# A streaming encoder step: two token differences moved from GpSimd to VectorE, one weight sum moved from VectorE to adding DMAs, and the queues reordered around them

## The chip, the cores and the metric

One core of one Trainium2 chip runs the whole program. The metric is the device time of that core in microseconds; before the change the median of three runs is 1407.86 us. Times below that carry a position, such as 317.2, are microseconds from the first instruction of one profiled execution.

## What is computed

Two layers of a hybrid encoder are applied to 640 tokens: 512 frames of one new stream and 16 frames of each of 8 running streams. All data is float32. Cut to what matters here:

```python
def hybrid_layer(x, ...):
    n = rms_norm(x, ln1_w)
    proj = n @ w_in                       # retention and short convolution use slices of proj
    ...
    x = x + concat([ret_out, conv_out]) @ w_out
    h2 = rms_norm(x, ln2_w)
    x = x + square(relu(h2 @ w_up)) @ w_down     # w_up (1024, 4096), w_down (4096, 1024)
    return x, r_new, new_buf
```

The change lies where the second half of a layer begins: at the product with `w_out` (its end) and the first block of `h2 @ w_up`.

## The kernel before

Each matrix product runs on TensorE with operands split into a high and a low part (both fp32r), as three matmuls: high by high, high by low, low by high. ScalarE makes the high part by a copy, VectorE the low part by subtracting the high part from the raw data. So every operand passes ScalarE, then VectorE, then TensorE.

The products with `w_out`, `w_up` and `w_down` are done by blocks called **quads**: 1 for `w_out` (quad 0), then for each of four blocks b of 512 by 512 quarters an up quad (2b+1) and a down quad (2b+2). A quad has four raw weight quarters of 1 MB, named 11, 12, 21 and 22, in four slots of `raws`. It is multiplied in Winograd's form, with **seven** products and not eight, each of sums and differences of quarters. In order they are B11, B21, SUM_1112, SUM_111222, SUM_1222, B22, SUM_ALL. An **item** is one product's weight: item = 7 * quad + product. It is split in two halves h = 0, 1 (`weight_half(item, h)`: ScalarE at line 1141, VectorE at line 1755) into a ring of two places, so that item n may be written when product n - 2 has been multiplied. Items of the first up quad are 7 (B11), 8 (B21), 9 (SUM_1112), 10, 11, 12 and 13.

The sums of weights come about in two ways. `weight_sum` (line 1765) is a VectorE addition in place: 11 += 12 gives SUM_1112, then 11 += 22 gives SUM_111222. `add_onto` (line 1474) is a DMA issued by GpSimd that adds a quarter from memory onto one that lies in `raws`: 12 += 22 for SUM_1222, once SUM_1112 has been made of the raw 12, and 11 += 21 for SUM_ALL.

The token side of the first up quad needs sums too, made once per layer since all four blocks b share them. Each is a tile of 128 x 1280. The normalised tokens are turned by TensorE (`turn`, line 703), tile by tile, and read by ScalarE (lines 968 to 973) and VectorE (lines 1546 and 1548), which also makes the first difference `t_diff` (named s_raw in the profile, as the next three are). Then GpSimd makes the second difference `s2_raw` = t_diff - t11 (line 1488) and the third `t21` = t11 - t21 (line 1489), and VectorE the fourth, `s4_raw` (`last_difference`, line 1844). Each is split by `in_diff_hi_of(n)` on ScalarE (line 1230) and `in_diff_lo_of(n)` on VectorE (line 1854 for n = 0, line 1852 for the others), with n = 0, 1, 2, 3 for products SUM_1112, SUM_111222, SUM_1222 and B22.

TensorE runs `up_half` (line 808), 24 matmuls for each product and half. Before a half it waits for its weights (`half_lo`), for its tokens (`in_diff_lo`), and for its PSUM banks: SUM_1112's half h goes to the bank that B21's half h leaves, when VectorE has added that to `hidden` (`hidden_sum`, line 1780). Copies of products by ScalarE (`copy_product`, line 1163) free the others.

Each engine runs its own list in the order in which the code stands; nothing is reordered. The order in the first up quad is written out by hand, in the branch `b == 0` of `up` on ScalarE and on VectorE. On GpSimd it is the loop over quads, with the row factors of the tokens (`row_rstd`, lines 1371 and 1374) in quad 0. On SyncE each load of a quad's quarters waits for the last low part made of what lies in its slot.

## Time and profile before

| | us |
|---|---|
| median of 3 runs | 1407.86 |
| lowest and highest | 1407.82 and 1409.0 |
| the profiled execution | 1408.8 |
| its span, first to last instruction | 1407.1 |

The two layers run the same instructions; what happens at 317 us in the first stands at 1012 us in the second. A row of a timeline gives start, duration, engine, line, operation and count, and in brackets the idle time before it and what ended that. "PE" is TensorE's matmuls, "DVE" VectorE, "ACT" ScalarE, "POOL" GpSimd, "SPq" the queue of SyncE. Start to start, VectorE's instructions in a row come 0.08 us sooner than their durations add up to, since one begins while the one before it drains.

### The profile page before, as it was taken

The page shows a single profiled execution, that of the slowest core. Times are in us where ns is not written, and L with a number is a line of the kernel's source. Part 1 is how long each engine was busy: PE and PEld are TensorE (multiplying, and loading weights), DVE is VectorE, ACT ScalarE, POOL GpSimd, SP SyncE. Part 2 cuts the span into 40 slices and gives each one's busy share as a digit, 9 for nine tenths or more (in the row PEclk, how much of TensorE's full clock was granted, in tenths as well). Part 3 has the DMA queues.
Part 4 walks back from the last instruction along what each step waited for, and adds up shares of the span by engine and source line. Part 5 has one row for each costly group of instructions (what it writes and reads, how often), then busy time and mean ns, then how long its engine had stood idle before and what let it go on. Part 6 is the DMA issues. An engine that isn't in the chain of part 4 may idle for free.

```text
span 1407.1 us, 21462 instructions
## 1 busy us (share of the span) xinstructions
PE 1377.2 (98%) x7702; PEld 1236.7 (88%) x7702; DVE 947.0 (67%) x1144; ACT 618.1 (44%) x736; POOL 191.4 (14%) x193
## 2 busy tenths in 40 slices
PE   8999999998999999999999999999899999999997
PEld 6888999888889899899878889998798998998986
DVE  5336415988975966867861473278889678688586
ACT  5311221466636446446543012134574464464463
POOL 2343200021000000000032430000400000000001
PEclk9999999999999999999999999999999999999999
DMA  7424203525454645555142242054166455544623
GB/s 273 135 76 121 83 1 128 134 84 122 110 159 121 145 100 142 146 118 158 31 138 96 90 121 68 3 158 140 46 150 150 103 142 145 120 120 120 150 60 105
DMA packets 93728, 162.39 MB, mean 115 GB/s; under 512 B 3956, under 2 KB 21492, under 8 KB 93624
## 3 DMA queue, kind: packets, MB, share of 16 engines
q1 hardware_dynamic: 74472, 123.18, 26.0%
q0 software_dynamic: 19008, 37.75, 15.8%
q8 instruction: 66, 1.08, 0.3%
q14 instruction: 38, 0.31, 0.1%
q10 hardware_dynamic: 144, 0.07, 0.0%
HBM read 153.58 MB, written 7.41 MB: 114 GB/s over the span
## 4 chain that ended last, share of the span: by engine, by line
PE 94%; DVE 2%; issue 2%; ACT 1%; POOL 1%; DMA 0%; DVEq 0%; SPq 0%; POOLq 0%; ACTq 0%
PE pair L808 27%; PE pair L867 25%; PE pair L653 15%; PE pair L663 12%; PE pair L880 8%; PE pair L703 2%; PE pair L741 1%; PE pair L748 1%; PE pair L722 1%; DVE ring L1755 1%; DVE x L1801 1%; PE pair L726 1%; PE pair L731 1%; DMA w_raw<-in_w_in 0%; PE pair L734 0%
## 5 line engine op out<-in xcount | busy, mean ns | idle before, releaser
L808 PE MATMUL pair<-mlp_in_hi,ring 128*128 128x320 f32 x1792 | 400.1, 311 | 9.8 <-DVE hidden L1780 9.8
L1141 ACT ACTIVATE ring<-raws 128x1024 fp32r<-128x1024 f32 x248 | 259.8, 1057 | 290.1 <-PE pair L867 150.2
L867 PE MATMUL pair<-ring,a_ring 128*128 128x512 f32 x1632 | 380.4, 390 | 0.0
L1755 DVE TENSOR_TENSOR ring<-raws,ring 128x1024 fp32r<-128x1024 f32 x248 | 305.2, 1241 | 101.6 <-ACT ring L1141 100.1
L867 PEld LDWEIGHTS pair<-ring,a_ring 128*128 128x128 f32 x1632 | 305.5, 188 | 63.6
L808 PEld LDWEIGHTS pair<-mlp_in_hi,ring 128*128 128x128 f32 x1792 | 302.7, 189 | 11.2 <-DVE ring L1755 10.3
L808 PE MATMUL pair<-mlp_in_lo,ring 128*128 128x320 f32 x896 | 278.2, 310 | 0.0
L808 PEld LDWEIGHTS pair<-mlp_in_lo,ring 128*128 128x128 f32 x896 | 169.6, 189 | 0.2
L663 PE MATMUL pair<-norm_hi,ring 128*128 128x320 f32 x512 | 114.5, 310 | 0.0
L1801 DVE TENSOR_TENSOR x<-x,pair 128x512 f32<-128x512 f32 x160 | 103.3, 678 | 11.4 <-PE pair L867 11.4
L653 PE MATMUL pair<-ring,norm_hi 128*128 128x512 f32 x320 | 101.6, 399 | 3.2 <-DVE norm_lo L1563 3.1
L653 PE MATMUL pair<-pair_a,norm_hi 128*128 128x512 f32 x320 | 101.0, 397 | 0.0
L880 PE MATMUL pair<-ring,sample_mid_hi 128*128 128x512 f32 x304 | 94.6, 392 | 0.0
L1765 DVE TENSOR_TENSOR raws<-raws 128x1024 f32<-128x1024 f32 x72 | 87.1, 1221 | 4.2
L663 PEld LDWEIGHTS pair<-norm_hi,ring 128*128 128x128 f32 x512 | 85.8, 188 | 0.1
L663 PE MATMUL pair<-norm_lo,ring 128*128 128x320 f32 x256 | 79.1, 309 | 0.0
L1474 POOL DMA_DIRECT2D raws<-in_w_mlp_down x16 | 20.7, 1295 | 391.4 <-DVE raws L1765 226.0
L653 PEld LDWEIGHTS pair<-ring,norm_hi 128*128 128x128 f32 x320 | 59.5, 191 | 16.0 <-DVE norm_lo L1563 2.0
L653 PEld LDWEIGHTS pair<-pair_a,norm_hi 128*128 128x128 f32 x320 | 58.9, 188 | 12.3 <-issue 1.0
L880 PEld LDWEIGHTS pair<-ring,sample_mid_hi 128*128 128x128 f32 x304 | 57.1, 188 | 12.6
L1780 DVE TENSOR_TENSOR hidden<-hidden,pair 128x640 f32<-128x640 f32 x48 | 39.3, 818 | 41.6 <-PE pair L808 41.6
L1816 DVE TENSOR_TENSOR a_ring<-hidden,a_ring 128x1024 fp32r<-128x1024 f32 x50 | 60.9, 1218 | 4.1 <-ACT a_ring L1216 4.1
(153 smaller groups left out, 1686.2 us busy)
## 6 DMA issues: line engine op xcount, KB each, us to landing
raws<-in_w_mlp_up SPq DMA_DIRECT2D x32, 1024.0 KB, 5.3
raws<-in_w_mlp_down SPq DMA_DIRECT2D x32, 1024.0 KB, 5.0
w_raw<-in_w_in SPq DMA_DIRECT2D x27, 1024.0 KB, 6.1
raws<-in_w_mlp_up POOLq DMA_DIRECT2D x16, 1024.0 KB, 9.1
raws<-in_w_mlp_down POOLq DMA_DIRECT2D x16, 1024.0 KB, 8.8
raws<-in_w_out SPq DMA_DIRECT2D x8, 1024.0 KB, 8.4
past_state<-in_state_ret SPq DMA_DIRECT2D x8, 512.0 KB, 4.5
out_ret_s<-past_state SPq DMA_DIRECT2D x8, 512.0 KB, 4.9
```

What stands on the lines that cost most here:

```text
L653: mm = pe.matmul(out, act[a][:, k, tile * P:(tile + 1) * P], w_of(b, n), start=(n == 0 and m == 0), stop=(n == len(ks) - 1 and m == 2))
L663: mm = pe.matmul(out, w_of(chunk, k // 4, a)[:, k % 4, ft * P:(ft + 1) * P], norms[b][:, k, half * HALF:(half + 1) * HALF], start=(k == 0 ...
L703: mm = pe.transpose(out[:, i * P:(i + 1) * P], src[i], identity)
L808: mm = pe.matmul(out[:, n, 0:HALF], item_half(item, h, a)[:, k, n * P:(n + 1) * P], mlp_in[i][c][:, k], start=(i in (B11, B21, SUM_1112, B ...
L867: mm = pe.matmul(out[:], a_item[:, a, 2 * h + k, pair * P:(pair + 1) * P], item_half(item, h, c)[:, k], start=(i in (B11, B21, SUM_1112) a ...
L880: mm = pe.matmul(sample_bank[:], sample_mid[part][a][:, k], item_half(item, k // 2, c)[:, k % 2], start=(i in (B11, SUM_1222) and (k, m) = ...
L1141: nc.scalar.activation(item_half(item, h, 0), raw_half(quad, RAW_OF[i], h), ACT.Copy).then_inc(half_hi.sem, 1)
L1755: nc.vector.tensor_tensor(item_half(item, h, 1), raw_half(quad, RAW_OF[i], h), f(item_half(item, h, 0)), ALU.subtract).then_inc(half_lo.se ...
L1765: nc.vector.tensor_tensor(out, out, raw_half(quad, name, h), ALU.add).then_inc(weights_summed.sem, 1)
L1780: nc.vector.tensor_tensor(hh, hh, src, ALU.add).then_inc(hidden_summed.sem, 1)
L1801: nc.vector.tensor_tensor(xx, xx, src[:], op).then_inc(x_added.sem, 1)
L1816: nc.vector.tensor_tensor(a_ring[:, n % 2, 1], src, f(a_ring[:, n % 2, 0]), ALU.subtract).then_inc(a_lo.sem, 1)
```

## The change

1. `s2_raw` and `t21` are made by VectorE (`next_difference`, `third_difference`) and not by GpSimd.
2. For quad 1, product SUM_1112 alone, VectorE's two additions 11 += 12 go. GpSimd issues two DMAs (`add_half`) in their place, each adding half of quarter 12 (512 KB, rows of 256 floats) from memory onto the half of 11 in `raws`, once the B11 item's half has been split. Each half has a semaphore of its own, `first_summed`, on which ScalarE's `weight_half(9, h)` waits. The DMA 12 += 22 of quad 1, which had waited for the additions, now waits only until quarter 12 is loaded, and stands right behind the second half in the queue.
3. The first half's DMA stands between the row factors of tiles 2 and 3, the second's behind those of tile 4.
4. The lists of ScalarE and VectorE for the first up quad are reordered.

```diff
+BY_DMA = (1, SUM_1112)
@@ ScalarE, weight_half
+                    elif (quad, i) == BY_DMA:
+                        act.wait_ge(first_summed[h].sem, first_summed[h].at(layer, 16))
@@ ScalarE, up(0)
                         read_tile(3)
                         weight_half(item + 1, 1)
+                        weight_half(item + 2, 0)
                         read_tile(4)
                         in_diff_hi_of(0)
-                        weight_half(item + 2, 0)
+                        weight_half(item + 2, 1)
                         copy_product(b, B11, 1)
+                        weight_half(item + 3, 0)
                         in_diff_hi_of(1)
-                        weight_half(item + 2, 1)
-                        weight_half(item + 3, 0)
-                        in_diff_hi_of(2)
                         copy_product(b, SUM_1112, 0)
-                        copy_product(b, SUM_1112, 1)
                         weight_half(item + 3, 1)
+                        copy_product(b, SUM_1112, 1)
+                        in_diff_hi_of(2)
                         weight_half(item + 4, 0)
+                        weight_half(item + 4, 1)
@@ GpSimd
+                def add_half(h):
+                    quad, i = BY_DMA
+                    pool.wait_ge(half_lo.sem, half_lo.at(layer, 2 * (quad * PRODUCTS + B11) + h + 1))
+                    settle(pool)
+                    pool.dma_start(raw_half(quad, "11", h), quad_weights(layer, quad, "12")[:, :, h * 256:(h + 1) * 256],
+                                   accum_op=ALU.add).then_inc(first_summed[h].sem, 16)
                 for quad in range(QUADS):
-                    pool.wait_ge(weights_summed.sem, weights_summed.at(layer, sums_to(quad, SUM_1112, 1)))
+                    if quad == BY_DMA[0]:
+                        slot = slot_of(quad, "12")
+                        pool.wait_ge(slot_in[slot].sem, slot_in[slot].at(layer, 16 * (quad + 1)))
+                    else:
+                        pool.wait_ge(weights_summed.sem, weights_summed.at(layer, sums_to(quad, SUM_1112, 1)))
                     add_onto(quad, "12", "22", onto_12)
@@ GpSimd, in quad 0
-                        for t in range(NT):
+                        for t in range(3):
                             row_rstd(layer, NT, t)
-                        last = TURN["n2", NT - 1, 1]
-                        pool.wait_ge(turn_lo.sem, turn_lo.at(layer, split_turns_to(last)))
-                        nc.gpsimd.tensor_tensor(s2_raw[:], t_diff[:], t11[:], ALU.subtract).then_inc(s2_ready.sem, 1)
-                        nc.gpsimd.tensor_tensor(t21[:], t11[:], t21[:], ALU.subtract).then_inc(s3_ready.sem, 1)
+                        add_half(0)
+                        for t in range(3, NT):
+                            row_rstd(layer, NT, t)
+                        add_half(1)
@@ VectorE
+                def next_difference():
+                    nc.vector.tensor_tensor(s2_raw[:], t_diff[:], t11[:], ALU.subtract).then_inc(s2_ready.sem, 1)
+                def third_difference():
+                    dve.wait_ge(s2_ready.sem, s2_ready.at(layer, 1))
+                    nc.vector.tensor_tensor(t21[:], t11[:], t21[:], ALU.subtract).then_inc(s3_ready.sem, 1)
```

VectorE, the first up quad, from the factors applied to tokens of tile 3 on. The names: xn is a normalised tile, `ring<-raws,ring` a weight half, `raws<-raws` a weight sum, `hidden` a hidden sum, `s_raw<-...` a difference. Before:

```order
L1765 TENSOR_TENSOR raws<-raws 128x4x256
L1854 SCALAR_TENSOR_TENSOR mlp_in_lo<-s_raw_102,mlp_in_hi 128x1280
L1754 REGISTER_ALU
L1755 TENSOR_TENSOR ring<-raws,ring 128x1024
L1772 REGISTER_ALU
L1777 ISA
L1780 TENSOR_TENSOR hidden<-hidden,pair 128x2x320
L1765 TENSOR_TENSOR raws<-raws 128x4x256
```

and now, from the same place (behind the last piece read of tile 4):

```order
L1773 TENSOR_TENSOR ring<-raws,ring 128x1024
L1880 SCALAR_TENSOR_TENSOR mlp_in_lo<-s_raw_102,mlp_in_hi 128x1280
L1790 REGISTER_ALU
L1795 ISA
L1798 TENSOR_TENSOR hidden<-hidden,pair 128x2x320
L1772 REGISTER_ALU
L1773 TENSOR_TENSOR ring<-raws,ring 128x1024
L1780 REGISTER_ALU
L1783 TENSOR_TENSOR raws<-raws 128x4x256
L1790 REGISTER_ALU
L1795 REGISTER_ALU
L1798 TENSOR_TENSOR hidden<-hidden,pair 128x2x320
```

The first sum is gone, the weight half of item 9 stands ahead of the low part of the tokens, and both halves of item 9 stand ahead of the second hidden sum. The two differences follow behind these rows.

GpSimd, from the row factors of the last tile (`var`, `rstd`) on, before:

```order
L1371 TENSOR_SCALAR var<-sums 128x1 [waits squares]
L1373 REGISTER_ALU
L1374 TENSOR_TENSOR rstd<-var,minus_half 128x1 [waits eps_step]
L1487 ISA
L1488 TENSOR_TENSOR s_raw_103<-s_raw_102,t_72 128x1280 [waits turn_lo]
L1489 TENSOR_TENSOR s_raw_100<-t_72,s_raw_100 128x1280
L1478 REGISTER_ALU
L1474 ISA [waits weights_summed]
L1474 DMA raws<-in_w_mlp_up 128x4x512
```

and now:

```order
L1378 TENSOR_SCALAR var<-sums 128x1 [waits squares]
L1380 REGISTER_ALU
L1381 TENSOR_TENSOR rstd<-var,minus_half 128x1 [waits eps_step]
L1487 REGISTER_ALU
L1489 ISA [waits half_lo]
L1489 DMA raws<-in_w_mlp_up 128x4x256
L1495 ISA
L1481 ISA [waits slot_in1]
L1481 DMA raws<-in_w_mlp_up 128x4x512
```

The differences have left the list, and the second half's DMA and the whole quarter's stand next to each other. The lists of TensorE and SyncE are the same as before.

## Rows read from the trace of the kernel before

**Rows 1.** The page, part 1: busy time, share of the span, instructions.
```profile
PE 1377.2 (98%) x7702; PEld 1236.7 (88%) x7702; DVE 947.0 (67%) x1144; ACT 618.1 (44%) x736; POOL 191.4 (14%) x193
```

**Rows 2.** Waits of TensorE: us in total, times, longest.
```profile
PE pair L808 <- DVE hidden L1780: 9.8, 2, 4.9
```

**Rows 3.** Timeline of TensorE, first layer (columns as told above).
```profile
309.80 0.66 PE L703 MATMUL pair<-const,xn 128*128 128x128 f32 x4 [0.94 <-DVE s_raw L1548]
...
316.75 0.46 PE L808 MATMUL pair<-mlp_in_hi,ring 128*128 128x320 f32 x2
...
317.19 0.31 PE L808 MATMUL pair<-mlp_in_hi,ring 128*128 128x320 f32 x1
322.41 0.63 PE L808 MATMUL pair<-mlp_in_hi,ring 128*128 128x320 f32 x1 [4.91 <-DVE hidden L1780]
...
325.43 0.45 PE L808 MATMUL pair<-mlp_in_hi,ring 128*128 128x320 f32 x2
```

**Rows 4.** Timeline of TensorE, second layer: the same place.
```profile
1016.71 0.63 PE L808 MATMUL pair<-mlp_in_hi,ring 128*128 128x320 f32 x1 [4.91 <-DVE hidden L1780]
```

**Rows 5.** Windows: length; busy (count) of PE, PEld, DVE, ACT, POOL; clock; DMA.
```profile
322.41:325.43 3.02, 3.02 (x12) 3.02 (x13) 2.63 (x3) 1.06 (x1) 1.21 (x1) 0.52 0.02 5
...
1016.71:1021.81 5.10, 5.10 (x20) 5.10 (x20) 4.71 (x5) 1.56 (x2) 1.33 (x1) 0.52 0.26 35
```

**Rows 6.** Timeline of VectorE, first layer, 304 to 318 us.
```profile
304.14 1.28 DVE L1528 SCALAR_TENSOR_TENSOR xn<-x,rstd,norm_row 128x1024 f32<-128x1024 f32 x1 [0.71 <-POOL rstd L1374]
306.13 1.28 DVE L1528 SCALAR_TENSOR_TENSOR xn<-x,rstd,norm_row 128x1024 f32<-128x1024 f32 x1 [0.71 <-POOL rstd L1374]
...
311.74 0.68 DVE L1548 TENSOR_TENSOR s_raw<-s_raw,pair 128x512 f32<-128x512 f32 x1
...
313.76 3.98 DVE L1854 SCALAR_TENSOR_TENSOR mlp_in_lo<-s_raw,mlp_in_hi 128x1280 fp32r<-128x1280 f32 x1 [0.21 <-ACT mlp_in_hi L1230]
317.66 3.89 DVE L1755 TENSOR_TENSOR ring<-raws,ring 128x1024 fp32r<-128x1024 f32 x1
```

**Rows 7.** Timeline of GpSimd, first layer, 294 to 325 us.
```profile
294.14 0.54 POOL L1374 TENSOR_TENSOR rstd<-var,minus_half 128x1 f32<-128x1 f32 x1
...
304.19 1.28 POOL L1371 TENSOR_SCALAR var<-sums 128x1 f32<-128x1 f32 x1
305.56 0.54 POOL L1374 TENSOR_TENSOR rstd<-var,minus_half 128x1 f32<-128x1 f32 x1
312.49 3.89 POOL L1488 TENSOR_TENSOR s_raw<-s_raw,t 128x1280 f32<-128x1280 f32 x1 [6.40 <-DVE s_raw L1548]
316.35 4.12 POOL L1489 TENSOR_TENSOR s_raw<-t,s_raw 128x1280 f32<-128x1280 f32 x1
324.22 1.33 POOL L1474 DMA_DIRECT2D raws<-in_w_mlp_up  x1 [3.75 <-DVE raws L1765]
```

**Rows 8.** Groups of VectorE, 300 to 345 us: busy, mean ns; idle.
```profile
L1765 DVE TENSOR_TENSOR raws<-raws 128x1024 f32<-128x1024 f32 x4 | 4.9, 1217 | 0.0
...
L1844 DVE SCALAR_TENSOR_TENSOR s_raw<-t,s_raw 128x1280 f32<-128x1280 f32 x1 | 1.5, 1485 | 0.0
```

**Rows 9.** Timeline of ScalarE, first layer, 307 to 313 us.
```profile
307.24 1.06 ACT L1141 ACTIVATE ring<-raws 128x1024 fp32r<-128x1024 f32 x1
...
312.45 1.28 ACT L1230 ACTIVATE mlp_in_hi<-s_raw 128x1280 fp32r<-128x1280 f32 x1 [1.35 <-DVE s_raw L1548]
```

**Rows 10.** Timeline of SyncE's queue, 311 us.
```profile
311.03 27.12 SPq L505 DMA_DIRECT2D raws<-in_w_mlp_down  x2
```

**Rows 11.** DMA issues: KB, median us to landing; then line 1474's.
```profile
raws<-in_w_mlp_up POOLq DMA_DIRECT2D x16, 1024.0 KB, 9.1
...
DMA to landing us min/median/max: 8.3/9.1/15.1
```

**Rows 12.** DMA queues, 326:334 and 141:145: packets, MB, share of 16.
```profile
q0 software_dynamic: 528, 1.05, 77.7%
...
q1 hardware_dynamic: 1040, 0.52, 46.0%
```

More of the change, by code:

```diff
@@ L419, in program @@
         half_lo = Signal("half_lo", 2 * ITEMS)
-        weights_summed = Signal("weights_summed", QUADS * len(SUMS))
+        weights_summed = Signal("weights_summed", QUADS * len(SUMS) - 2)
+        first_summed = [Signal(f"first_summed{h}", 16) for h in range(2)]
         onto_12 = Signal("onto_12", 16 * QUADS)
```

31 lines of the change are left out of this document (16 added, 15 removed).

## The prediction

> **What bounds the kernel.** Read the busy shares first: TensorE is busy for 98% of the span, all others far less [rows 1], so only time in which TensorE stands still, or runs slowly, can be won. Next its waits: one pair stands out, 9.8 us in two waits of 4.9, on VectorE's hidden sum [rows 2]. Then its timeline around each. In both layers TensorE ends B21 and stands before SUM_1112's first half. In the first layer the last matmul starts at 317.19, one more would have started at 317.34 (three take 0.44, from 316.75 to 317.19), and the next comes at 322.41: 5.07 us lost [rows 3]; the second layer has the same 4.91 us of idle [rows 4]. Then come slow matmuls: 11 start from 322.41 until 325.43 (the window counts 12, one of them the one before the edge or at it), and 19 from 1016.71 until 1021.81, at a mean clock of 0.52, nearly all at the lower of its two levels (1.2 GHz) [rows 3, 4, 5]. At 0.147 us each they would take 1.61 and 2.79 us, and they take 3.02 and 5.10, so 1.41 and 2.31 us more. Before it stood still the engine had run at that full pace. The whole price of the place is 2 x 5.07 + 1.41 + 2.31 = **13.86 us**.
>
> **Why VectorE is late there.** Its low part of t_diff took 3.98 us and the weight half behind it 3.89 [rows 6]. The same instruction form on the same shape takes 1.49 [rows 8], and a weight half has the shape and operands of a sum, 1.22 [rows 8]. During both, GpSimd made its two differences, 312.49 to 320.47 [rows 7]. The times fit turns taken, not shared: 316.38 (GpSimd's end) + 1.49 = 317.87, against 317.74 measured. So 2.49 + 2.67 = 5.16 us of VectorE's time is waiting for GpSimd, and a sum of 1.22 stood ahead of them.
>
> **What the change takes off and puts on VectorE**, per layer: off two sums, 2 x 1.22 = 2.44, and the 5.16 of waiting; on two differences of 1.49 each (two inputs of 128 x 1280, priced by the nearest row, the fourth difference, line 1844 [rows 8]), 2.98. Net 4.6 us less, and what is added stands behind what TensorE waits for first.
>
> **The new order followed through the first layer.** I use starts, each step being its duration less 0.08: weight half or sum 1.14, low part or difference 1.40, hidden sum 0.73 (the form takes about 0.81), half a read of a turned tile 0.60.
>
> Tile 3 is normalised at 304.14 [rows 6]; now the weight half (8, 0) follows at 305.34. GpSimd's factor for tile 4 was computed at 305.56 while VectorE idled [rows 6, 7]; its forerunner, begun at 304.19, took 1.28 us beside a VectorE instruction [rows 7]. So I take it that the factor now waits until 306.5 and ends at 307.05, and that tile 4 is normalised at 307.2, not 306.13. Tile 3's low parts start at 308.4 and 309.0. TensorE's last turn waits for the second of them: it started at 309.80 [rows 3], now at 309.73. Tile 4's low parts start at 311.06 and 311.67, against 311.74 for the second [rows 6]. This stretch gains 0.07 us; if the factor slips in earlier, it gains up to 0.3.
>
> Then VectorE: weight half (9, 0) at 312.3; low part of t_diff at 313.7 (ScalarE's high part starts 0.71 behind 311.67, at 312.4, and takes 1.28 [rows 9]); hidden sum 0 at 315.1; weight half (9, 1) at 315.8; sum at 317.0; hidden sum 1 at 318.1, behind B21's second half (its last matmul starts at 317.1); second difference at 318.8; weight half (10, 0) at 320.2; low part 1 at 321.7; sum at 323.1; third difference at 324.2; weight half (10, 1) at 325.6; low part 2 at 327.1; (11, 0) at 328.5.
>
> TensorE, if never stopped, starts SUM_1112's halves at 317.3 and 320.8, SUM_111222's at 324.3 and 327.8, SUM_1222 at 331.4 (24 matmuls of 0.147 are 3.52 us). What each needs is done at 315.9, 318.9, 323.1, 326.8 and 329.7. The margins are 1.4, 1.9, 1.2, 1.0 and 1.7 us, and by the same steps B22, due at 338.4, has its tokens at 335.4. So the stall goes whole, unless a DMA is late. What is late next is VectorE's (10, 1), with 1.0 us.
>
> **The two adding DMAs.** The first half is issued behind tile 2's factor, which ends at 294.68 [rows 7], with nothing to stop tile 3's factor at 303; it may take the longest landing seen, 15.1 us [rows 11], and be there at 311. ScalarE reaches it at 308.2, behind the half that started at 307.24 [rows 9]. At the median it costs nothing. Its ends: 0, or up to 2.5 us of ScalarE, with tile 4's reads queued behind it.
>
> The second half decides. Tile 4's factor ends at 307.05. A release came 0.8 us before the DMA's start in the one row that shows it (a sum ended at 323.4, the DMA started at 324.22 [rows 7]), so it starts at about 307.9. ScalarE waits for it with (9, 1), and behind that wait stand its copy of B11 and all of SUM_111222's weights; VectorE's queue waits with it. Weight half (9, 1) at 315.8 wants it landed by **314.6**; with the margin of 1.0, TensorE loses nothing up to **315.6**, and one us for each beyond. No row shows an adding DMA of 512 KB. Upper end: as long as the whole, 9.1 us [rows 11], plus contention with SyncE's load issued at 311.03 [rows 10], taken as 1.5: landed at 318.5. Lower end: packets cost by size. An adding packet of 2 KB costs 0.777 x 16 x 8 / 528 = 0.188 us, 33 per engine 6.2 us; a plain one of 512 B costs 0.46 x 16 x 4 / 1040 = 0.028 us, and a plain one of 2 KB some 0.09 (half the 0.188, since adding reads the destination too: an estimate from these two rows) [rows 12]. So cost goes by size, half the bytes take 3.1 us less, and 9.1 becomes 6.0: landed at 313.9. I take 6 to 7, landed at 314 to 315, since the packet rows are nearest. No stall.
>
> This change splits one large transfer where there was none. The Trainium skill, "DMA: Bandwidth & Descriptors", "Anatomy of one DMA — SWDGE (gpsimd) path", speaks against small ones: a fixed 2.0 us and then bytes at 436 GB/s, which makes 512 KB cost 0.73 of 1 MB. On the 9.1 us measured that would be 6.6 us, landed at 314.5, by an estimate from that page; its own figure for 1 MB, 4.4 us, is half of what this trace has for an adding DMA, so the trace does not agree with its size.
>
> The DMA 12 += 22 now goes out at 309.2 and not at 324.22 [rows 7]; it is wanted at 327. It costs nothing unless it shares the queue with the half in front of it (below).
>
> **The sum.** 1408.8 of the profiled execution - 13.9 = 1394.9. The median lies 0.9 under that execution, so **1394.0**, 0.98% less.
>
> **Rivals.**
>
> *The half is late, or VectorE is over its margins* (0.20). Either the DMA lands at 316 to 318.5, or a step is dearer than priced. One way is that the 3.98 us is this instruction's own cost, with its factor of -1 and fp32r output, and not GpSimd's doing: 2.49 us more, less 1.0 of margin, is 1.5 a layer. Against it: line 1844 has two inputs and such a factor at 1.49 [rows 8]. With the DMA at its upper end it is 318.5 - 315.6 = 2.9 a layer. That gives 1394.0 + 3.0 to 5.8 = 1397 to 1399.8.
>
> *The same time as before* (0.04). A landing at 321 gives back what is won.
>
> *Slower* (0.04). The half and the 1 MB behind it in GpSimd's queue are drained together, not one after the other. Then the half lands with the whole: 307.9 + 9.1 + 3.1, and 3 us more for SyncE's load, is 323. TensorE then stands for 7.4 us where it stood for 5.07, with the same slow clock behind: +2.3 a layer, so 1407.9 + 4.6 = 1412.5. It decides from a landing at about 320.7. For it: no row shows two of GpSimd's DMAs one right behind the other, and one alone took 15.1 [rows 11]. Against it: the half is 1.3 us ahead, the time its descriptors take to be written [rows 7].
>
> **Chances.** Stall gone whole: 0.70, 1393 to 1395.5. Late or dear: 0.20. As before: 0.04. Slower: 0.04. The rest, 0.02, is a wait elsewhere, of which I see none, since all later work hangs on TensorE's pace. What a measurement of this kernel can tell from no change is about 0.2%, 2.8 us. Faster 0.92, same 0.04, slower 0.04. The range reaches up over most of the second case, 1398.5, and down to 1392.8, for the turns' waits (0.94 us a layer [rows 3]) falling with the rest.
>
> **What would show it.** Right: no wait of TensorE on line 1780's successor, no stretch at half clock near 322 and 1016 less the shift, low part of t_diff at 1.5 us, second half's landing before 315.6, both differences at 1.4 to 1.5 us on VectorE. Wrong: a TensorE wait behind ScalarE's weight half (9, 1), which is the DMA; a wait at SUM_111222, which is VectorE's load; a VectorE instruction there still near 4 us, which is a GpSimd instruction or something else holding it.

## The result

The changed kernel takes **1393.47 us** (median of 4 runs, 1393.14 to 1394.05), against 1408.43 for the kernel before in the runs beside it (4 runs, 1407.82 to 1413.44). The ratio is **0.9888 [0.987, 0.9905]**: faster by 1.1%. The forecast was 0.98% (1394.0 of 1407.86, a ratio of 0.9902). It lies within the interval of the ratio. But the ratio times 1407.86 is 1392.1, and that lies 0.7 us below the low end of the range, 1392.8. How far outside depends on one run: the median itself, 1393.47, lies inside the range, and the kernel before has a run of 1413.44 beside three of 1407.82 to 1409.0. The quotient of the two medians is 0.9894; that of the means is 0.9887, and 0.9896 without that run, which would be 1393.2. The direction and the mechanism hold. The gain is larger than the sum's 13.9 us, by 1.1 us between the medians (14.96) and by 1.9 us by the ratio.

The profiled execution of the changed kernel took 1394.05; its span is 1392.4, 14.7 less than before.

### The profile after

The page of the changed kernel, part 1 (busy time, share of the span, instructions), to be laid beside [rows 1]:

```profile
PE 1372.0 (99%) x7702; PEld 1232.0 (88%) x7702; DVE 937.7 (67%) x1144; ACT 617.5 (44%) x736; POOL 182.4 (13%) x193
```

TensorE's waits in the changed kernel, over the whole span (us in total, times, longest). The group of [rows 2], 9.8 us in two waits, is gone, and nothing of the first up quad has taken its place; what is left there is the wait for the turned tiles, on line 1566. Three of the five rows:

```profile
PE pair L644 <- DMA x<-in_x_sample: 4.9, 1, 4.9
PE pair L658 <- DVE norm_lo L1581: 3.4, 2, 2.1
PE pair L708 <- DVE s_raw L1566: 2.3, 4, 0.6
```

VectorE's timeline in the changed kernel, first layer, from the weight half (9, 0) on (start, duration, engine, line, operation, count, and in brackets the idle time before it with what ended that). Line 1773 is the weight half, 1880 and 1878 are the low parts of the tokens, 1860 and 1865 the two differences that came from GpSimd:

```profile
311.36 1.22 DVE L1773 TENSOR_TENSOR ring<-raws,ring 128x1024 fp32r<-128x1024 f32 x1
312.79 1.49 DVE L1880 SCALAR_TENSOR_TENSOR mlp_in_lo<-s_raw,mlp_in_hi 128x1280 fp32r<-128x1280 f32 x1 [0.21 <-ACT mlp_in_hi L1237]
...
315.23 1.23 DVE L1773 TENSOR_TENSOR ring<-raws,ring 128x1024 fp32r<-128x1024 f32 x1 [0.21 <-ACT ring L1148]
...
318.24 1.49 DVE L1860 TENSOR_TENSOR s_raw<-s_raw,t 128x1280 f32<-128x1280 f32 x1
...
321.07 1.49 DVE L1878 TENSOR_TENSOR mlp_in_lo<-s_raw,mlp_in_hi 128x1280 fp32r<-128x1280 f32 x1 [0.21 <-ACT mlp_in_hi L1237]
...
323.62 1.48 DVE L1865 TENSOR_TENSOR s_raw<-t,s_raw 128x1280 f32<-128x1280 f32 x1
```

The low part of t_diff takes 1.49 where it took 3.98, the weight half behind it 1.23 where it took 3.89 [rows 6], and the two differences cost 1.49 and 1.48. No instruction here is near 4 us.

GpSimd's timeline in the changed kernel, first layer: the factors of tile 4, the second half's adding DMA (line 1489), and the whole quarter's (line 1481):

```profile
303.48 1.29 POOL L1378 TENSOR_SCALAR var<-sums 128x1 f32<-128x1 f32 x1
304.85 1.41 POOL L1381 TENSOR_TENSOR rstd<-var,minus_half 128x1 f32<-128x1 f32 x1
306.22 1.34 POOL L1489 DMA_DIRECT2D raws<-in_w_mlp_up  x1
314.35 1.29 POOL L1481 DMA_DIRECT2D raws<-in_w_mlp_up  x1 [6.78 <-issue]
```

The DMA 12 += 22 was expected right behind the half, at about 309. It went out at 314.35, after 6.78 us in which GpSimd waited for nothing that the profile names.

ScalarE's weight half (9, 1), which waits for the second half's DMA, in the first and the second layer of the changed kernel:

```profile
314.13 1.06 ACT L1148 ACTIVATE ring<-raws 128x1024 fp32r<-128x1024 f32 x1 [1.38 <-DMA raws<-in_w_mlp_up]
```

```profile
1002.53 1.06 ACT L1148 ACTIVATE ring<-raws 128x1024 fp32r<-128x1024 f32 x1 [2.01 <-DMA raws<-in_w_mlp_up]
```

So the DMA did end last there, and two views show how close it came. The first is the line of landings of line 1489 in the changed kernel; the second is TensorE's timeline in the second layer, at the matmul where SUM_111222 begins:

```profile
DMA to landing us min/median/max: 6.2/7.1/8.4
```

```profile
1011.03 0.58 PE L813 MATMUL pair<-mlp_in_hi,ring 128*128 128x320 f32 x2
1011.45 0.31 PE L813 MATMUL pair<-mlp_in_lo,ring 128*128 128x320 f32 x1
```

A pair of such matmuls spans 0.46 elsewhere; this one spans 0.58, so TensorE stood for 0.12 us in the middle of it. The landing 8.4 us after the issue in the second layer just used the margin up. In the first layer it landed after 7.8 us, and nothing was lost.

### Where the 14.7 us went

A layer's first up quad is measured from its first matmul to the first matmul of the down quad behind it. For the changed kernel these are two rows of TensorE's timeline, the first and the last of the stretch:

```profile
299.52 0.41 PE L813 MATMUL pair<-mlp_in_hi,ring 128*128 128x320 f32 x1
...
351.56 0.39 PE L872 MATMUL pair<-ring,a_ring 128*128 128x512 f32 x1
```

and for the kernel before:

```profile
300.25 0.41 PE L808 MATMUL pair<-mlp_in_hi,ring 128*128 128x320 f32 x1
...
359.00 0.63 PE L867 MATMUL pair<-ring,a_ring 128*128 128x512 f32 x2
```

The same two places of the second layer stand at 987.30 and 1039.46 in the changed kernel, at 994.55 and 1054.22 in the one before.

| us | before | changed | less |
|---|---|---|---|
| first up quad, layer 1 | 58.75 | 52.04 | 6.71 |
| first up quad, layer 2 | 59.67 | 52.16 | 7.51 |
| from the start to the first of them | 300.25 | 299.52 | 0.73 |
| between them | 635.55 | 635.74 | -0.19 |
| behind them | 352.88 | 352.94 | -0.06 |

The two quads give 14.22. The 0.73 at the start is not the change's: the two programs run the same work there, and a second profile of the kernel before (below) has its first up matmul at 299.49, as early as the changed kernel. In the first profile of before, TensorE ran a stretch from 10 to 16 us at a mean granted clock of 0.72, in that of the changed kernel at 1.00. Windows (length; busy and count of PE, PEld, DVE, ACT, POOL; clock; DMA share; GB/s), before and then changed:

```profile
10.00:16.00 6.00, 5.17 (x20) 4.20 (x20) 5.33 (x8) 4.33 (x9) 1.64 (x3) 0.72 1.04 405
```

```profile
10.00:16.00 6.00, 4.55 (x23) 3.64 (x24) 5.38 (x8) 4.45 (x9) 1.65 (x3) 1.00 1.04 407
```

### The profile page after: what moved, and what is told of

Its sections match the earlier page's. It is cut to its first block, busy times and chain, and to the rows that moved or that the text cites. A ratio compares the mean times of both kernels' runs of the same rounds, so it can differ in the third digit from the quotient of the medians.

```text
span 1392.4 us, 21466 instructions
## 1 busy us (share of the span) xinstructions
PE 1372.0 (99%) x7702; PEld 1232.0 (88%) x7702; DVE 937.7 (67%) x1144; ACT 617.5 (44%) x736; POOL 182.4 (13%) x193
## 3 DMA queue, kind: packets, MB, share of 16 engines
HBM read 155.67 MB, written 7.41 MB: 117 GB/s over the span
## 4 chain that ended last, share of the span: by engine, by line
PE 94%; issue 2%; DVE 1%; ACT 1%; POOL 1%; DMA 0%; DVEq 0%; SPq 0%; POOLq 0%; ACTq 0%
PE pair L813 27%; PE pair L872 26%; PE pair L658 15%; PE pair L668 12%; PE pair L885 8%; PE pair L708 2%; PE pair L746 1%; PE pair L753 1%; PE pair L727 1%; PE pair L731 1%; PE pair L736 1%; DVE x L1819 0%; DMA w_raw<-in_w_in 0%; PE pair L739 0%; POOL var L1378 0%
## 5 line engine op out<-in xcount | busy, mean ns | idle before, releaser
L1773 DVE TENSOR_TENSOR ring<-raws,ring 128x1024 fp32r<-128x1024 f32 x248 | 300.1, 1221 | 96.5 <-ACT ring L1148 95.1
L1783 DVE TENSOR_TENSOR raws<-raws 128x1024 f32<-128x1024 f32 x68 | 82.3, 1223 | 4.2
L658 PEld LDWEIGHTS pair<-pair_a,norm_hi 128*128 128x128 f32 x320 | 58.9, 188 | 12.3 <-issue 1.0
```

The costliest lines, as they stand in the source:

```text
L658: mm = pe.matmul(out, act[a][:, k, tile * P:(tile + 1) * P], w_of(b, n), start=(n == 0 and m == 0), stop=(n == len(ks) - 1 and m == 2))
L1773: nc.vector.tensor_tensor(item_half(item, h, 1), raw_half(quad, RAW_OF[i], h), f(item_half(item, h, 0)), ALU.subtract).then_inc(half_lo.se ...
L1783: nc.vector.tensor_tensor(out, out, raw_half(quad, name, h), ALU.add).then_inc(weights_summed.sem, 1)
```

## The experiments

Each is told with its sections: the length of the first up quad in layers 1 and 2, measured as above. "Stall" is an idle time of TensorE in that quad, other than the wait for a turn. Each ratio is against runs of the kernel before that were taken with it on the same chip.

### Both kernels again

> The changed kernel once more, more rounds, to narrow its ratio. Theory A (the gain is the stall at SUM_1112, 13.9 us, plus about 0.5 us of shorter turn waits; the rest of the 14.7 us between the two spans is the start of the program, where the trace of before shows matmuls at the lower clock from 11.4 to 14.8 us and that of the changed kernel none): ratio 0.9893 to 0.9900 where both start alike. Rival B (the change itself gives 15.5 us or more): 0.9888 again.

> The kernel before, unchanged. Theory A: the 3.4 us of lower clock at 11.4 us come and go from run to run; a second profile has the first up matmul anywhere between 299.5 and 300.3 us, and a ratio of 1.000. Rival B: the dip at the start is the same each time, at 300.25 us.

The changed kernel took 1394.78 (1393.39 to 1396.61), the ratio is 0.99 [0.9884, 0.9917]; the one before 1409.05, ratio 1.0007 [0.9997, 1.0017]. This interval holds the ratios of both theories; what decides for the first is the start, 299.49 us, with a clock of 1.00 from 10 to 16 us. The sections of the changed kernel are 52.03 and 52.03, those of before **59.38 and 59.95**, where its first profile had 58.75 and 59.67. The stalls are the same, 4.92 and 4.91. What differs is the slow stretch around the end of the stall. A window of the kernel before, run again, over the stall of layer 1 and what follows; then the same window of its first profile:

```profile
317.00:328.00 11.00, 6.34 (x30) 6.35 (x31) 10.61 (x8) 2.80 (x3) 4.04 (x2) 0.69 0.23 37
```

```profile
317.00:328.00 11.00, 6.09 (x33) 5.83 (x32) 10.61 (x8) 2.73 (x4) 4.80 (x2) 0.84 0.17 24
```

The mean granted clock is 0.69 and not 0.84. The lower level is half of the upper one, so a mean of 0.69 is 2 x 0.31 x 11 = 6.8 us of the 11 at the lower level, where there were 3.5. Part of it lies in the stall itself, where it costs nothing: 2.5 of the 6.8, and 0.5 of the 3.5. Of the rest, 16 matmuls from 321.65 to 326.02 took 4.37 us for 2.35. So the term of 1.41 us of slow matmuls in layer 1, from [rows 5], is 2.02 here, and layer 2's, by its 22 matmuls, is 2.59 against 2.31. By this profile the price of the place is 14.8 us, not 13.86.

The changed kernel's run had a slow stretch too, in another place, in the second layer's first products. Windows of it and of the first profile of the changed kernel:

```profile
705.00:712.00 7.00, 5.87 (x23) 4.82 (x24) 3.84 (x6) 0.79 (x2) 1.42 (x2) 0.76 0.74 270
```

```profile
705.00:712.00 7.00, 6.21 (x31) 5.26 (x32) 4.97 (x7) 2.12 (x4) 1.74 (x4) 1.00 0.70 255
```

It made the way between the two up quads 637.47 instead of 635.74: 1.7 us, with nothing changed in the program.

### Each part alone

The differences on VectorE alone, with the DMAs and sums as before and the lists reordered only around them (the functions `next_difference` and `third_difference` as in the change; GpSimd's two differences removed):

```diff
@@ ScalarE
                         copy_product(b, B11, 1)
-                        in_diff_hi_of(1)
                         weight_half(item + 2, 1)
                         weight_half(item + 3, 0)
-                        in_diff_hi_of(2)
+                        in_diff_hi_of(1)
                         copy_product(b, SUM_1112, 0)
-                        copy_product(b, SUM_1112, 1)
                         weight_half(item + 3, 1)
+                        copy_product(b, SUM_1112, 1)
+                        in_diff_hi_of(2)
@@ VectorE
                         weight_sum(q, SUM_111222, 0)
-                        in_diff_lo_of(1)
+                        next_difference()
                         weight_half(item + 3, 0)
+                        in_diff_lo_of(1)
                         weight_sum(q, SUM_111222, 1)
+                        third_difference()
                         weight_half(item + 3, 1)
```

> The two differences on VectorE, the weight sums left on VectorE as before. By VectorE's steps the low part of the first difference takes 1.49 us, TensorE starts SUM_1112 without a stall (at most 0.2 us), but SUM_111222 waits about 1.8 us a layer for the low part of the second difference: 2 x (6.9 - 1.9) = 10 us saved, 1398 us, ratio 0.993. Rival (the 3.98 us belong to the instruction): low part still near 4 us, ratio 0.997 or more.

1399.85 (1398.05 to 1404.5), ratio 0.9943 [0.9925, 0.9962]; sections 54.22 and 54.22. TensorE's wait before SUM_1112 is gone. One is left, before SUM_111222: first TensorE's waits, then what VectorE did, in the first layer.

```profile
PE pair L808 <- DVE mlp_in_lo L1855: 1.7, 1, 1.7
```

```profile
312.88 1.49 DVE L1857 SCALAR_TENSOR_TENSOR mlp_in_lo<-s_raw,mlp_in_hi 128x1280 fp32r<-128x1280 f32 x1 [0.21 <-ACT mlp_in_hi L1230]
...
323.60 1.49 DVE L1855 TENSOR_TENSOR mlp_in_lo<-s_raw,mlp_in_hi 128x1280 fp32r<-128x1280 f32 x1 [0.21 <-ACT mlp_in_hi L1230]
```

The low part is short at once, at 1.49. Behind it VectorE now has both its own sums and GpSimd's differences, and the second low part comes 1.7 us late. No slow stretch follows. The median lies 1.9 us over the expected 1398, and in the profiled execution the way between the two up quads is 637.44 us, 1.9 us longer than in the first profile of before.

The DMAs and the new order alone, with the differences left to GpSimd:

```diff
                         add_half(1)
+                        last = TURN["n2", NT - 1, 1]
+                        pool.wait_ge(turn_lo.sem, turn_lo.at(layer, split_turns_to(last)))
+                        nc.gpsimd.tensor_tensor(s2_raw[:], t_diff[:], t11[:], ALU.subtract).then_inc(s2_ready.sem, 1)
+                        nc.gpsimd.tensor_tensor(t21[:], t11[:], t21[:], ALU.subtract).then_inc(s3_ready.sem, 1)
@@ VectorE
-                        next_difference()
...
-                        third_difference()
```

> The adding DMAs and the new order, the two differences left on GpSimd. If VectorE and GpSimd take turns, the low part of the first difference takes 3.8 to 4 us again, TensorE stalls about 1.1 us before SUM_1112's first half and 1.4 before its second: 9.3 us saved, 1399 us, ratio 0.9935. If the DMA sum were the main thing: 0.990.

1399.75 (1399.02 to 1402.58), ratio 0.9943 [0.9926, 0.9959]; sections 54.87 and 54.87. TensorE stands for 1.09 and 1.23 us in each layer. VectorE's timeline has the two held instructions:

```profile
312.98 3.98 DVE L1886 SCALAR_TENSOR_TENSOR mlp_in_lo<-s_raw,mlp_in_hi 128x1280 fp32r<-128x1280 f32 x1 [0.21 <-ACT mlp_in_hi L1237]
...
317.61 3.22 DVE L1778 TENSOR_TENSOR ring<-raws,ring 128x1024 fp32r<-128x1024 f32 x1
```

Against the first profile of before, 4.5 and 5.5 us of the two sections go by the first part alone, 3.9 and 4.8 by the second alone, and 6.7 and 7.5 by both: the two gains overlap, and neither part alone clears the place.

### Both parts, but the old order

ScalarE's and VectorE's lists in the first up quad are those of before, with the two differences put between the hidden sums and behind the second sum of SUM_111222. Cut to the moves that the rows below turn on:

```diff
@@ ScalarE
                         weight_half(item + 1, 1)
-                        weight_half(item + 2, 0)
                         read_tile(4)
                         in_diff_hi_of(0)
-                        weight_half(item + 2, 1)
+                        weight_half(item + 2, 0)
                         copy_product(b, B11, 1)
-                        weight_half(item + 3, 0)
                         in_diff_hi_of(1)
+                        weight_half(item + 2, 1)
+                        weight_half(item + 3, 0)
@@ VectorE
-                        weight_half(item + 2, 0)
                         in_diff_lo_of(0)
+                        weight_half(item + 2, 0)
                         hidden_sum(b, B21, 0)
+                        next_difference()
+                        hidden_sum(b, B21, 1)
                         weight_half(item + 2, 1)
                         weight_sum(q, SUM_111222, 0)
-                        hidden_sum(b, B21, 1)
-                        next_difference()
-                        weight_half(item + 3, 0)
                         in_diff_lo_of(1)
+                        weight_half(item + 3, 0)
```

> Both parts of the change, but ScalarE's and VectorE's lists in the order of the kernel before (each difference where its next reader wants it). By the same steps: a stall of 1.3 us before SUM_1112's second half (its weights stand behind the high part of the second difference on ScalarE) and about 4 before SUM_111222's second half: 1405 us, ratio 0.998. If the order is worth little, 1394 us.

1408.74 (1405.27 to 1409.56), ratio **0.9994** [0.9984, 1.0004], sections 59.04 and 59.05: nothing is left of the gain. TensorE's waits in the first up quad of one layer, and ScalarE's timeline there:

```profile
PE pair L813 <- DVE ring L1773: 4.5, 2, 3.4
```

```profile
318.18 1.28 ACT L1237 ACTIVATE mlp_in_hi<-s_raw 128x1280 fp32r<-128x1280 f32 x1 [3.28 <-DVE s_raw L1860]
319.36 1.04 ACT L1148 ACTIVATE ring<-raws 128x1024 fp32r<-128x1024 f32 x1
...
327.90 1.27 ACT L1237 ACTIVATE mlp_in_hi<-s_raw 128x1280 fp32r<-128x1280 f32 x1 [3.93 <-DVE s_raw L1865]
```

The weight half (9, 1) stands behind the high part of the second difference in ScalarE's list. It starts at 319.36, though its DMA had landed by 314.5, where GpSimd issued the next: ScalarE waits 3.28 us in its queue for VectorE to make a difference that TensorE needs only one product later. The half (10, 1) stands in the same way behind the high part of the third difference, for which ScalarE waits 3.93 us, and TensorE stalls 3.44 us before SUM_111222's second half. The stalls, 1.06 and 3.44, add up to about the one of before. The median is 3.7 us over the expected 1405; in both layers TensorE ran slowly behind the longer stall (a mean clock of 0.68 from 332.61 to 336.00).

### Only the length of GpSimd's work

This is the kernel before with one edit that speaks on the mechanism alone: GpSimd still issues both instructions, at the same point, but over one column. It leaves out the rest of both differences, so its outputs are not those of the layer; the second product's tokens and the fourth difference read `t_diff` in place of `s2_raw`, so VectorE and ScalarE do the same amount of work as before.

```diff
-                        nc.gpsimd.tensor_tensor(s2_raw[:], t_diff[:], t11[:], ALU.subtract).then_inc(s2_ready.sem, 1)
-                        nc.gpsimd.tensor_tensor(t21[:], t11[:], t21[:], ALU.subtract).then_inc(s3_ready.sem, 1)
+                        nc.gpsimd.tensor_tensor(s2_raw[:, 0, 0:1], t_diff[:, 0, 0:1], t11[:, 0, 0:1], ALU.subtract).then_inc(s2_ready.sem, 1)
+                        nc.gpsimd.tensor_tensor(t21[:, 0, 0:1], t11[:, 0, 0:1], t21[:, 0, 0:1], ALU.subtract).then_inc(s3_ready.sem, 1)
```

> The kernel before with GpSimd's two differences cut to one column each (the rest of them is left out, and the second one's readers take the first difference), so that GpSimd holds nothing; VectorE's list, its sums and its order are those of before. If GpSimd's 8 us beside VectorE are the whole cause, the low part of the first difference takes 1.49 us, TensorE has no stall over 0.3 us in the first up quad, and first up matmul to first down matmul takes 52.3 us a layer: 1394 us. If VectorE's sums or the order were part of the cause in themselves, 2 us or more of stall stay: 1398 us or more.

1394.12 (1393.77 to 1397.47), ratio **0.9894** [0.9878, 0.9911], sections 52.40 and 52.39, no stall. VectorE's and GpSimd's rows:

```profile
312.46 1.22 DVE L1765 TENSOR_TENSOR raws<-raws 128x1024 f32<-128x1024 f32 x1
313.89 1.49 DVE L1854 SCALAR_TENSOR_TENSOR mlp_in_lo<-s_raw,mlp_in_hi 128x1280 fp32r<-128x1280 f32 x1 [0.20 <-ACT mlp_in_hi L1230]
315.29 1.22 DVE L1755 TENSOR_TENSOR ring<-raws,ring 128x1024 fp32r<-128x1024 f32 x1
```

```profile
312.62 1.11 POOL L1488 TENSOR_TENSOR s_raw<-s_raw,t 128x1 f32<-128x1 f32 x1 [6.40 <-DVE s_raw L1548]
313.69 0.18 POOL L1489 TENSOR_TENSOR s_raw<-t,s_raw 128x1 f32<-128x1 f32 x1
```

With VectorE's sum still ahead of the low part, in the old order, without any DMA of halves, the stall is gone whole (52.3 is what the changed kernel takes with the old wait for the turn, below). **The stall was GpSimd's doing**, all 5 us of it. The sums are free as long as VectorE is not held. This edit also makes GpSimd's results ready at once, and by itself it does not tell a held VectorE from late results. The rows do: in the kernel before the second difference was ready at 316.38 [rows 7], and here ScalarE's weight half (9, 1) waits for VectorE's sum until 318.4 anyway. So it was the holding. GpSimd's first instruction also shows the reverse: one column takes 1.11 us when it is issued under VectorE's sum, and ends at 313.73 with it (313.68); the next takes 0.18.

### GpSimd's work moved by one instruction

The kernel before, with the two differences held until VectorE's first low part is made:

```diff
-                        pool.wait_ge(turn_lo.sem, turn_lo.at(layer, split_turns_to(last)))
+                        pool.wait_ge(in_diff_lo.sem, in_diff_lo.at(layer, 1))
```

> The kernel before with GpSimd's two differences held until the low part of the first one is made. If an instruction that begins first keeps the other out until its end, the low part takes 1.49 us and SUM_1112's first half starts without a stall, but the sum or weight half beside each of GpSimd's instructions takes about 2.5 us more, and TensorE stalls about 3 us before SUM_1112's second half, whose weights stand on ScalarE behind the high part of the second difference: 2 to 4 us a layer saved, 1402 us. If the slow instruction is slow by itself, 1408 us and a low part of 4 us.

1404.79 (1402.32 to 1405.63), ratio 0.9964 [0.995, 0.9978], sections 57.24 and 55.93, a stall of 3.16 before SUM_1112's second half. VectorE's rows and GpSimd's:

```profile
313.12 1.49 DVE L1854 SCALAR_TENSOR_TENSOR mlp_in_lo<-s_raw,mlp_in_hi 128x1280 fp32r<-128x1280 f32 x1 [0.20 <-ACT mlp_in_hi L1230]
...
316.40 3.25 DVE L1765 TENSOR_TENSOR raws<-raws 128x1024 f32<-128x1024 f32 x1
319.57 0.81 DVE L1780 TENSOR_TENSOR hidden<-hidden,pair 128x640 f32<-128x640 f32 x1
320.85 2.64 DVE L1755 TENSOR_TENSOR ring<-raws,ring 128x1024 fp32r<-128x1024 f32 x1 [0.47 <-ACT ring L1141]
```

```profile
314.69 3.87 POOL L1488 TENSOR_TENSOR s_raw<-s_raw,t 128x1280 f32<-128x1280 f32 x1 [9.22 <-DVE mlp_in_lo L1854]
318.53 3.88 POOL L1489 TENSOR_TENSOR s_raw<-t,s_raw 128x1280 f32<-128x1280 f32 x1
```

The low part, the same instruction with its factor and fp32r output, is at 1.49 as soon as no difference runs beside it, and now the plain sum is the one that takes 3.25. The times are those of turns: GpSimd's first ends at 318.56 less some 0.1, plus 1.22, is 319.7 (the sum ends at 319.65); its second ends at 322.41, plus 1.22 is 323.6 (323.49). GpSimd takes turns too: its second difference, recorded from 318.53, stood under the sum until 319.65 and then took 2.8 us, as did the two of the kernel before, counted from the end of the VectorE instruction in front of each (a sum that ended at 313.55, and the low part at 317.74; they end at 316.38 and 320.47). The hidden sum between them, one of whose inputs lies in PSUM, keeps its 0.81 beside a running difference. The Trainium skill, "SBUF — State Buffer", "Who interferes with whom", states this: a VectorE instruction with two SBUF inputs contends with a GpSimd instruction that reads SBUF; one with at most one SBUF input, outside VectorE's 2-port modes, does not; and the shared ports are an exclusive lock, which whoever issues first has for the whole instruction (the page says the last of the 2-port modes). These rows agree with all three.

Of the 3.16 us, some 1.4 are VectorE's second wait (2.64 for 1.22). The rest comes by ScalarE's weight half (9, 1), which starts only at 319.78: it had to wait for the sum, held until 319.65, and for the high part of GpSimd's late difference in front of it, begun at 318.60. The median lies 2.8 us over the expected 1402; behind the stall there was a slow stretch in layer 1 and none in layer 2, whose section is 1.3 us shorter.

### The adding DMAs

The whole quarter's DMA issued ahead of the second half's, which makes the half as late as the slower rival has it:

```diff
                             row_rstd(layer, NT, t)
+                        slot = slot_of(1, "12")
+                        pool.wait_ge(slot_in[slot].sem, slot_in[slot].at(layer, 32))
+                        add_onto(1, "12", "22", onto_12)
                         add_half(1)
```

> The changed kernel with GpSimd's two neighbouring DMAs swapped: the whole quarter (12 += 22) is issued ahead of the second half, so the half is late. GpSimd stood 6.8 to 7.4 us in the changed kernel before its next DMA; if it is held until the DMA in front has landed, the half starts at about 315.6 and lands at 322 to 324, TensorE stalls 7 to 9 us a layer and runs at half clock after it: 1413 us, slower than before (ratio 1.000 to 1.006). If GpSimd is not held, the half starts at 307.6 and lands by 319: a stall of 4 to 5 us, 1404 us.

1416.58 (1412.22 to 1417.81; 1413 was expected), ratio **1.005** [1.0032, 1.0069], sections 63.03 and 61.84, stalls 7.96 and 8.15. GpSimd's rows, and ScalarE's:

```profile
307.12 1.34 POOL L1481 DMA_DIRECT2D raws<-in_w_mlp_up  x1
318.26 1.29 POOL L1489 DMA_DIRECT2D raws<-in_w_mlp_up  x1 [9.80 <-issue]
```

```profile
324.60 1.06 ACT L1148 ACTIVATE ring<-raws 128x1024 fp32r<-128x1024 f32 x1 [10.95 <-DMA raws<-in_w_mlp_up]
```

The price of a late half is as the forecast had it. It gave one us for each us behind a landing of 315.6, and with a landing at 324.5 that is 8.9. But the stall stands before SUM_1112's second half, whose margin was put at 1.9 and not 1.0, so 8.0, and 7.96 idle came. The half is late for another reason than thought, though: it was not drained together with the whole, it was not even issued until the whole had landed, 10.8 us after its start.

So the same kernel as the changed one, with the memory reserved for the descriptors of such DMAs one step larger:

```diff
-    nc = bacc.Bacc("TRN2", target_bir_lowering=False, num_devices=1, dynamic_dma_scratch_size=2048)
+    nc = bacc.Bacc("TRN2", target_bir_lowering=False, num_devices=1, dynamic_dma_scratch_size=2112)
```

> The changed kernel with 2112 bytes and not 2048 of scratch for GpSimd's DMA descriptors, nothing else. Theory: GpSimd is held before the whole quarter's DMA for want of descriptor space; with 64 bytes more that DMA starts at 307.6, 6.7 us sooner. If the queue is drained in order, the half still lands at 314 and the time is that of the changed kernel, 1393.5 us. Rival of the prediction (both drained together): the half lands at 317 to 319 and TensorE stalls 3 us a layer, 1400 us. If space is not the cause, the DMA still starts at 314.35.

1394.47 (1393.88 to 1395.67), ratio 0.9902 [0.9886, 0.9919], sections 52.03 and 52.33. GpSimd's rows, then the DMAs issued from 305 to 330 (KB, median us to landing):

```profile
307.14 1.33 POOL L1489 DMA_DIRECT2D raws<-in_w_mlp_up  x1
307.95 1.85 POOL L1481 DMA_DIRECT2D raws<-in_w_mlp_up  x1
```

```profile
raws<-in_w_mlp_up POOLq DMA_DIRECT2D x2, 1024.0 KB, 12.3
raws<-in_w_mlp_down SPq DMA_DIRECT2D x1, 1024.0 KB, 13.4
raws<-in_w_mlp_up POOLq DMA_DIRECT2D x1, 512.0 KB, 8.2
```

The hold is gone with 64 bytes more: the whole quarter's DMA goes out 0.81 us behind the half's. The half lands 8.2 us after its issue, against 7.8 in the same layer of the changed kernel, and the whole 15.9 us after its own (the 12.3 is the median of this and a later one of 8.8), 8.5 us behind the half. So the queue was drained in its order here, and not both together. In the first layer the 0.4 us cost nothing (52.03), in the second 0.3 us (52.33). As for the time, the larger memory brings nothing, since nobody wants the whole quarter before 327.

### The weight half put ahead of tile 4's normalisation

```diff
                         normalise(layer, NT, 3, ORDER[3], 32)
-                        weight_half(item + 1, 0)
                         normalise(layer, NT, 4, ORDER[4], 32)
+                        weight_half(item + 1, 0)
```

> The changed kernel with tile 4 normalised ahead of weight half (8, 0), as before. One look, by the profile: if the 0.24 us a layer of shorter turn wait come from this exchange, TensorE idles 0.94 us before its last turn again (0.54 in the changed kernel) and first up matmul to first down matmul takes 52.3 us, not 52.05.

One execution, 1393.92, sections 52.30 and 52.29 where the changed kernel has 52.04 and 52.16. The wait for the last turn is 0.95 again, as in [rows 3], not 0.54. This edit of the order is worth 0.25 us a layer, which no measurement of the whole kernel here can tell.

## Why the prediction was right, and where it was not

**What bounds the kernel, and why VectorE was late:** right. The stall, its 5.07 us a layer and the slow matmuls behind it went whole; that this price was taken from too few rows is told below. The reading of 3.98 and 3.89 us as turns taken with GpSimd is shown by the runs with one column and with GpSimd held, and the rival that 3.98 was the instruction's own cost is refuted by the 1.49 of every run that had no difference beside it.

**The prices of the new work:** right. The two differences were put at 1.49 each, from [rows 8], and took 1.49 and 1.48. Step by step the chain came as it was written: the forecast's starts, less the 0.73 by which this execution was ahead, lie within 0.3 us of the rows. The low part of t_diff comes at 312.79 for 313.7 - 0.73 = 312.97, the second difference at 318.24 for 318.07, the third at 323.62 for 323.47.

**The turn gain, 0.07 us a layer:** too small, and left out of the sum, whose 13.9 is the 13.86 of the stall and the slow matmuls alone. TensorE's last turn began at 308.83, which is 9.31 behind its first up matmul at 299.52; it was 309.80 - 300.25 = 9.55 before. That is 0.24, inside the "up to 0.3" that the text allowed if the factor slipped in. The factor did take its turn behind the weight half (1.41 us, 304.85 to 306.26, forecast 307.05 - 0.73 = 306.32); but VectorE took up the normalisation at 306.30 and not at 306.47.

**The second half's DMA:** two steps were wrong and made up for each other. Its issue was put at 307.9, 0.8 us behind the release, from the one row in [rows 7] that had a release to measure. It started at 306.22, right behind the factor, 0.95 earlier than 307.9 - 0.73. And it took 7.8 and 8.4 us, not 6 to 7. The step "cost goes by size", with its 6.0, is near the least that such a half took, 6.2. What was missing in the likeliest value was most likely SyncE's loads, which the forecast counted in its upper end alone: the first halves, issued with no such load beside them, took 6.3 and 6.2, and in the run with the whole quarter first the second halves, issued when those loads were nearly in, took 6.2 and 6.5. No run took the loads away from the second half. The loads are the other issues from 305 to 316:

```profile
raws<-in_w_mlp_down SPq DMA_DIRECT2D x1, 1024.0 KB, 7.0
...
norm_row<-in_norm_rows SPq DMA_DIRECT2D x1, 512.0 KB, 6.5
```

The landing, 306.22 + 7.8 = 314.0, is at the late end of the forecast's 313.3 to 314.3 in this frame. The threshold held to 0.2 us: 315.6 was forecast, 314.9 in this frame, less 0.2 for the earlier turn, so 314.7. The second layer's landing, 994.00 + 8.4 = 1002.4, answers to 1002.4 - (987.30 - 299.52) = 314.6 and lost 0.12 us; the first layer's lost nothing. What came due first was not the weight half (10, 1) but, as far as the rows tell, the low part of the second difference: in layer 2 it ended at 1010.96, 0.3 before the matmul that was late (1011.30), and in layer 1 at 322.56, 0.8 before the same matmul.

**The DMA 12 += 22:** "issued at 309.2" was wrong, and the slower rival's mechanism with it. GpSimd was held 6.78 and 7.41 us behind the half. It cost nothing because it was wanted at 327 and GpSimd had nothing else to do. The rival's price was real, as the run with the whole quarter first shows (1.005); its condition, that both are drained together, came about neither here nor with the larger memory. The rival counted the half 1.3 us ahead; with the larger memory the next DMA started 0.81 us behind it.

**The sum, and the step that failed:** the two sections gave 6.71 and 7.51. The forecast's terms were 5.07 + 1.41 + 0.07 = 6.55 and 5.07 + 2.31 + 0.07 = 7.45. With 0.24 for the turn, and 0.12 taken off in layer 2, they come to 6.72 and 7.50, which is what was measured to 0.01 us. So in the profiled execution the only mis-sized term of the place is the turn gain: 0.48 us where the sum had nothing. The other mis-sized term is the **price of the slow matmuls**: 1.41 + 2.31 = 3.72 was read from one execution, [rows 3 to 5], and another execution of the same kernel has 2.02 + 2.59 = 4.61. It varies by about 1 us, was taken as fixed, and was taken from its cheap side. The later runs point the same way: the three with a stall over 3 us came 2.8 to 3.7 us over their expected times, in which the slow clock was priced low or not at all; the four others for which a time was expected came 0.1 to 1.9 over.

How much of the excess in the medians is this term is not shown, since only two executions of the kernel before have a profile. 13.9 + 0.9 for it, + 0.5 for the turns and - 0.1 for layer 2 is 15.2; the medians of pairs run side by side differ by 14.96 in the first set, 13.08 in the second, and 14.8 for the kernel with one column. That the first is near 15.2 is in part luck.

**The range** was the other failure. Its low end took in 1.2 us, for the turns' waits, and nothing for this term nor for the stretches at lower clock elsewhere: 0.73 at 10 us in the execution that the sum was made against, 1.7 at 707 us in one of the changed kernel. The way between the two up quads, which no edit here touches, takes 635.0 to 636.1 us in eight of the twelve profiles and 637.4 to 638.3 in the other four. Medians of the kernel before are 1407.86 and 1409.05 (14 and 10 runs on one chip), 1409.02 (14) and 1408.89 (8) on two others. A low end of 1391.9, lower by the 0.9 us of the slow matmuls, would have been worked out by an estimate from the second profile. The ratio of the second set, 0.99, would give 1393.8, inside the range: the result stands at the edge of what the runs can tell from the forecast.

**The chances:** 0.70 for the stall gone whole is the case that came; the median of 1393.47 lies in its 1393 to 1395.5, the 1392.1 of the ratio does not. The 0.20 for a late half was not idle, since its margin in layer 2 was below zero by 0.12 us.

## What to carry to other kernels

When two neighbouring rows of VectorE take three times what the same form takes elsewhere, look for GpSimd's instructions beside them and add up its end and their own length; if it fits, move the work by who holds whom, not by who has time left. Removing waits or work from an engine can bring nothing if a list in program order still puts a thing due later ahead of a thing due now: the same two parts gave 1.1% in the new order and nothing in the old. And where a stall's price has a term for the slow clock behind it, read it from both layers and every profile there is, and give the range its spread.

## What the runs showed of the hardware

- The stretch at the lower clock around the end of a stall varies between executions of one kernel: 3.5 us in one and 6.8 in the other at the same stall of 4.9 us in layer 1, with 0.5 and 2.5 us of them inside the stall. Behind stalls of 1.1 to 1.7 us no slow stretch was seen in these runs; behind one of 3.16 there was one in layer 1 and none in layer 2; behind one of 3.44 there was one in both; at 8.0, one of some 10.3, 4.1 of it inside the stall.
- TensorE also ran slow stretches of some 3.4 us at 10 us or at 707 us, where other executions of the same program had none, with waits in front of them that differed by at most 0.3 us. In the profiles of the runs with the whole quarter first, with the larger memory and with one column, the first up matmul came at 300.4 too, and only 20 matmuls ran from 10 to 16 us, though their rows show a clock of 1.00 there: the rows of the clock do not show every slow stretch.
- With 2048 bytes reserved, no adding DMA of GpSimd's went out in these stretches before the one in front had landed, and with that DMA next in its list GpSimd stood still for 6.8 to 9.8 us; with 2112 it went out after 0.8 us. The profile calls this idle time "issue". Other work was not held: in the run with the differences left on GpSimd the first of them started at 311.73, 5.3 us behind the half's DMA.
- An adding DMA of 512 KB, in rows of 1 KB, landed after 6.2 to 6.5 us with little beside it and after 7.8 to 8.6 beside SyncE's loads. One of 1 MB took 9.1 at the median of before, 10.8 where it lay against those loads, and 15.9 right behind a half.
- GpSimd's differences of 128 x 1280 were recorded with 3.9 to 4.2 us, of which some 2.8 were their own and the rest waiting for VectorE: the recorded duration of either engine's instruction holds the time for which the other kept it out.
